# A two-block model kernel: reordering of the first stage (state-space tables, attention heads, modulation weights)

## The reference, cut to what matters

```python
mod = silu(c) @ mod_w[0] + mod_b[0]            # 1024 -> 6*1024
sh1, sc1, g1, sh2, sc2, g2 = split(mod, 6)
h = rms_norm(x, norm_g[0, 0]) * (1 + sc1) + sh1
proj = h @ ab_w_in[0]                          # u (512) and q, k, v (8 heads of 64)
# S5, 2048 complex states: A = exp(dt * a)
#   state[t] = A * state[t-1] + B u[t];  y = Re(C state) + d*u;  y = gelu(y) * sigmoid(...)
# attention: softmax(q k^T / 8 + bias) v, causal, one block of 256
x = x + g1 * (concat(y_ssm, y_att) @ ab_w_out[0])
```

## Time and profile before

| | us |
|---|---|
| median of 3 runs | 1697.28 (1697.18 to 1698.23) |
| the profiled execution, its own time | 1699.96 |
| its span on the core | 1698.2 |
| mean granted TensorE clock | 0.941 |
| front, up to the first product of ab_in | 0 to 51 |
| ab_in loop | 51 to 139 |
| head loop | 139 to 202 |
| glu chunk begins in earnest | 208.86 |

### The profile page before, as it was taken

How to read it: one execution, slowest core, us unless ns; L and a number is a source line. 1 busy time by engine, 2 the same in 40 slices (tenths; PEclk the granted TensorE clock), 3 DMA queues, 4 the chain that set the end, 5 groups by cost and what they waited for, 6 DMA issues and landing times.

```text
span 1698.2 us, 29024 instructions
## 1 busy us (share of the span) xinstructions
PE 1546.5 (91%) x11142; PEld 1395.4 (82%) x11142; DVE 1259.4 (74%) x2002; ACT 746.4 (44%) x987; POOL 52.1 (3%) x38
## 2 busy tenths in 40 slices
PE   4598889999889899999968899889999899889998
PEld 1584479999889799999968565689999778889997
DVE  7998658888989847888964488567666678576665
ACT  2223445444453225444444656454545533254543
POOL 2401100000000000000000000000000000000000
PEclk8698999999999789999979979999999999999999
DMA  8325719878623318777524366435555332235551
GB/s 339 130 94 203 293 50 365 303 289 316 250 88 122 124 50 323 302 303 297 184 108 144 104 213 229 167 115 183 179 191 210 137 124 100 84 123 190 175 195 49
DMA packets 54036, 316.23 MB, mean 186 GB/s; under 512 B 6503, under 2 KB 7560, under 8 KB 28808
## 3 DMA queue, kind: packets, MB, share of 16 engines
q1 hardware_dynamic: 52120, 310.79, 50.2%
q10 hardware_dynamic: 1840, 4.41, 0.9%
HBM read 312.56 MB, written 1.05 MB: 185 GB/s over the span
## 4 chain that ended last, share of the span: by engine, by line
PE 73%; DVE 14%; DMA 4%; issue 4%; ACT 4%; DVEq 1%; POOL 0%; ACTq 0%
PE bank L1841 62%; DMA arena<-in_mod_stream 3%; DVE arena L1143 3%; PE bank L1781 2%; DVE hf L1583 2%; PE bank L2038 2%; DVE rstd L1258 1%; DVE hf L1276 1%; PE bank L2062 1%; PE bank L1795 1%; DVE h_lo L1286 1%; DVE w_lo L1109 1%; ACT w_hi L667 1%; PE bank L1892 1%; PE bank L1807 1%
## 5 line engine op out<-in xcount | busy, mean ns | idle before, releaser
L1841 PE MATMUL bank<-h_hi,w_hi 128*128 128x256 f32 x2184 | 640.6, 293 | 62.1 <-DVE h_lo L1286 55.3
L1841 PE MATMUL bank<-h_lo,w_hi 128*128 128x256 f32 x2184 | 629.2, 288 | 0.0
L1841 PE MATMUL bank<-h_hi,w_lo 128*128 128x256 f32 x2184 | 628.6, 288 | 0.0
L1109 DVE TENSOR_TENSOR w_lo<-raw,w_hi 128x2048 fp32r<-128x2048 f32 x186 | 426.5, 2294 | 135.7 <-ACT w_hi L667 134.9
L1841 PEld LDWEIGHTS bank<-h_hi,w_hi 128*128 128x128 f32 x2184 | 430.3, 197 | 76.1 <-issue 60.3
L1841 PEld LDWEIGHTS bank<-h_lo,w_hi 128*128 128x128 f32 x2184 | 431.1, 197 | 1.1 <-issue 0.7
L1841 PEld LDWEIGHTS bank<-h_hi,w_lo 128*128 128x128 f32 x2184 | 430.6, 197 | 0.0
L667 ACT ACTIVATE w_hi<-raw 128x2048 fp32r<-128x2048 f32 x186 | 355.3, 1911 | 161.9 <-PE bank L1841 152.4
L1841 PE MATMUL bank<-a_hi,w_hi 128*128 128x256 f32 (+1 forms) x760 | 221.6, 292 | 9.9 <-DVE a_lo L1286 3.7
L1841 PE MATMUL bank<-a_lo,w_hi 128*128 128x256 f32 (+1 forms) x760 | 219.3, 289 | 0.0
L1841 PE MATMUL bank<-a_hi,w_lo 128*128 128x256 f32 (+1 forms) x760 | 219.1, 288 | 0.0
(11 more groups left out here) (257 smaller groups left out, 1575.6 us busy)
## 6 DMA issues: line engine op xcount, KB each, us to landing
raw<-in_stream SPq DMA_DIRECT2D x186, 1024.0 KB, 4.9
arena<-in_mod_stream SPq DMA_DIRECT2D x96, 768.0 KB, 6.1
raw<-in_mod_pe SPq DMA_DIRECT2D x36, 512.0 KB, 6.7
arena<-in_ctx_mod SPq DMA_DIRECT2D x8, 1024.0 KB, 5.9
arena<-in_mod_pe SPq DMA_DIRECT2D x12, 512.0 KB, 12.6
sq<-in_bias SPq DMA_DIRECT2D x8, 256.0 KB, 7.2
x<-in_x_t ACTq DMA_DIRECT2D x1, 1024.0 KB, 9.2
arena<-in_ctx_t SPq DMA_DIRECT2D x1, 1024.0 KB, 4.7
```

The lines of the kernel that those rows point to most:

```text
L1109: nc.vector.tensor_tensor(w_lo[s][:], raw[s][:], w_hi[s][:].bitcast(F32), ALU.subtract).then_inc(lo_done, 1)
L1841: ins = nc.tensor.matmul(out_, l, r, start=first and n == 0, stop=last and n == 2, **kw)
```

## The change

1. **Table by recurrence, and on VectorE alone.** `e_pair` now builds only steps 0 to 127 by six instructions over 256 elements. Steps 128 to 255 come from E[t] = 2 cos(64 * angle) * E[t-64] - E[t-128], in four instructions over 128 elements each. The powers shrink with it (six squarings instead of seven, `e1` to 8 entries). All eight pairs are VectorE's: 0 and 1 ahead of the ab_in loop, 2, 3 and 4 at c = 2, 4, 6, and 5, 6 and 7 at h = 1, 3, 5.
2. **All 16 sine products on GpSimd.** `ssm_tile` of tiles 0 to 7 loses L1326; `turned_back(c-1)` comes ahead of `ssm_tile(c)`, and `y_of` has two products for every tile.
3. **Modulation in thirds.** Pieces 0 to 15 as before; 16 to 31 during the ab_in loop, in `hf` and `sq`, two per chunk (four at c = 7); 32 to 47 in the heads, three per head. The bias tiles share `sq` and so are loaded after piece 31. VectorE reads vectors 2 and 3 (`first_mod_out(2, 4)`) between the loops, and `scores(0)` waits for that, since they lie in its bank.
4. **Head step.** VectorE: `head(h)` first, then `ssm_tile(8+h)`, a pair, `recip(h)`, `turned_back(8+h)`. TensorE: `scores(h+1)` first. ScalarE: `probs(h)` at the end of step h.

```diff
         def e_pair(v, link, g):
...
-            v.tensor_tensor(er, a[0], b[0], ALU.mult)
-            link(v.tensor_tensor(part, a[1], b[1], ALU.mult))
-            link(v.tensor_tensor(er, er, part, ALU.subtract))
...
+            er, ei = (t[:, j, 0:T // 2].rearrange("p j (a b) -> p j a b", b=16) for t in (e_re, e_im))
...
+            for q in (2, 3):
+                for k in range(2 * g, 2 * g + 2):
+                    e = [e_all[:, :, k, 64 * (q - i):64 * (q - i) + 64] for i in range(3)]
+                    ins = v.scalar_tensor_tensor(e[0], e[1], cols_[:, 12, k:k + 1], e[2], ALU.mult, ALU.subtract)
+                link(ins)
...
         def _(pool):
-            for g in range(E_POOL, ST // 2):
-                e_pair(nc.gpsimd, link, g).then_inc(sem("e_ready"), 1)
-                pool.wait_ge(sem("e_ready"), g - E_POOL + 1)
-            for j in range(8, ST):
-                pool.wait_ge(sem("scan_done"), j - 7)
+            for j in range(ST):
+                pool.wait_ge(sem("scan_done"), j + 1)
+                if j >= 2:
+                    pool.wait_ge(sem("state_ready"), j - 1)
                 nc.gpsimd.tensor_tensor(by_sin[j % 2], rot_b, e_im[:, j, :].unsqueeze(1).broadcast_to([P, 2, T]), ALU.mult)\
...
             for c in range(8):
                 lo_upto(Q["ab_in"] + c + 3)
+                if c:
+                    turned_back(c - 1)
                 ssm_tile(c)
-                if c in (2, 4):
-                    link(e_pair(nc.vector, link, 1 + c // 2))
-                if c == 6:
-                    y_out(0)
+                if c in (2, 4, 6):
+                    e_pair(nc.vector, link, 1 + c // 2)
+            y_out(0)
+            turned_back(7)
+            first_mod_out(2, 4)
             for h in range(HEADS):
-                if h % 2 == 0:
-                    dve.wait_ge(sem("e_ready"), h // 2 + 1)
+                head(h)
+                if h == 1:
+                    y_out(1)
                 ssm_tile(8 + h)
-                if h == 0:
-                    y_out(1)
+                if h in (1, 3, 5):
+                    e_pair(nc.vector, link, 5 + h // 2)
                 if h == 5:
                     y_out(2)
-                if h == HEADS - 1:
-                    turned_back(8 + h)
-                if h:
-                    recip(h - 1)
-                head(h)
-                if h < HEADS - 1:
-                    turned_back(8 + h)
-            recip(HEADS - 1)
+                recip(h)
+                turned_back(8 + h)
             y_out(3)
-            first_mod_out(2, 6)
+            first_mod_out(4, 6)
...
                 if c >= 2:
                     y_of(c - 2)
+                for m in beside_pieces(c):
+                    pm_piece(m)
+            pm_turn(3)
...
             pe.wait_ge(bank_free, FILL["ab_in"] + 8)
+            pe.wait_ge(sem("mod_read"), 2)
             scores(0)
             for h in range(HEADS):
+                if h + 1 < HEADS:
+                    scores(h + 1)
                 if h + 9 < ST:
                     bu(9 + h)
...
                 if h:
                     head_out(h - 1)
-                if h + 1 < HEADS:
-                    scores(h + 1)
```

More of the change, by code:

```diff
@@ L400, in build @@
             MOD_HALF.append((buf[j % n], landed[j % n], _n_[key], n))
-        pm_landed = [sem(f"pm_landed{i}") for i in range(PM_SLOTS)]
-        PM_PIECE, _n_ = [], [0] * PM_SLOTS
-        for m in range(PM_PIECES):
-            k = m % PM_SLOTS if m < PM_FIRST else (m - PM_FIRST) % PM_LATE
-            _n_[k] += 16
-            PM_PIECE.append(((pm_w if m < PM_FIRST else pm_late)[k], pm_landed[k], _n_[k]))
+        PM_PIECE, _n_ = [], {}
+        for first, last, ring in ((0, PM_FIRST, pm_w), (PM_FIRST, PM_BESIDE, pm_beside), (PM_BESIDE, PM_PIECES, pm_late)):
+            for m in range(first, last):
+                k = (m - first) % len(ring)
+                _n_[k] = _n_.get(k, 0) + 16
+                PM_PIECE.append((ring[k], sem(f"pm_landed{k}"), _n_[k], m - len(ring) + 1 if m >= first + len(ring) else None))
@@ L567, in _ @@
             sp.wait_ge(sem("h_ready"), H[1])
+            for m in range(PM_FIRST, PM_FIRST + 4):
+                load_pm(m)
+            for c, q in enumerate(range(Q["ab_in"] + 6, Q["ab_out"] + 2)):
+                load(q)
+                for m in (2 * c, 2 * c + 1):
+                    load_pm(PM_FIRST + 4 + m)
+            for m in range(PM_FIRST + 14, PM_BESIDE):
+                load_pm(m)
+            sp.wait_ge(sem("pm_used"), PM_BESIDE)
             for h in range(4):
                 load_bias(h)
-            load_plain("ab_in", 6)
-            load_plain("glu")
-            load_plain("ab_out", 0, 2)
             sp.wait_ge(hi_done, Q["ab_out"] + 2)
@@ L782, in _ @@
             for h in range(HEADS):
-                if h:
-                    probs(h - 1)
                 act.wait_ge(sem("peak_ready"), h + 1)
@@ L792, in _ @@
                     probs_copy(h - 1)
-                for g in range(2, 6):
+                for g in (4, 5):
                     if 8 * g + 7 in late_pieces(h):
@@ L797, in _ @@
                     head_copy(h - 1)
+                probs(h)
             for n in range(UT):
@@ L1215, in _ @@
             link(nc.vector.tensor_copy(pows[0][:, 1, :], sn))
-            for k in range(7):
+            for k in range(6):
                 p, p2 = pows[k], pows[k + 1]
@@ L1252, in first_mod_out @@
                 bias = par[:, COL["mod_b"] + c0:COL["mod_b"] + c1]
-                src = half(6, 0) if g0 == 0 else half(4, 1)
-                link(nc.vector.tensor_tensor(mod[:, 0, c0:c1], src[:, c0:c1], bias, ALU.add))
+                src = half(6, 0) if g0 == 0 else half(PM_SUM[g0], 1)
+                nc.vector.tensor_tensor(mod[:, 0, c0:c1], src[:, c0:c1], bias, ALU.add).then_inc(sem("mod_read"), 1)
+                dve.wait_ge(sem("mod_read"), g1 // 2)
             def norm_rstd(n):
@@ L1886, in y_of @@
                     pe.wait_ge(sem("y_ready"), n - 1)
-                c_, s_ = by_cos[j % 2], by_sin[j % 2]
-                terms = [(0, c_[:, 0, :]), (1, c_[:, 1, :])]
-                if j < 8:
-                    terms += [(2, s_[:, 1, :]), (1, s_[:, 0, :])]
-                for i, (e, v) in enumerate(terms):
-                    ins = nc.tensor.matmul(half(Y_BANK[n], 0)[r:r + 32, :], c_turned[:, e, n, r:r + 32], v, start=(i == 0), stop=(i == len(terms) - 1))
+                for e in range(2):
+                    ins = nc.tensor.matmul(half(Y_BANK[n], 0)[r:r + 32, :], c_turned[:, e, n, r:r + 32], by_cos[j % 2][:, e, :],
+                                           start=(e == 0), stop=(e == 1))
                 ins.then_inc(sem("ssm_y_done"), 1)
```

86 lines of the change are left out of this document (37 added, 49 removed).

## The result

The changed kernel took 1707.68 us (median of 13 runs, 1703.06 to 1711.39). The kernel before took 1698.23 us on the same chip (median of 13, 1689.49 to 1704.46). The ratio is 1.0053, with a 95% interval of 1.0036 to 1.007: slower by about 9 us, where 1698.1 with a range of 1691 to 1706 was predicted. The profiled execution took 1708.16 us with a span of 1706.3, so its numbers are set against the 1699.96 and 1698.2 of before.

The account below looks back on a forecast made before the run. VectorE was taken to bound both loops; 16.6 us gained in front were given back as four more pairs (15.2), stalls (9.5) and combining, less savings. Glu comes 0.7 us later, 209.6 against 208.86; total 1698.1 us, range 1691 to 1706.

Parts of the forecast that it names:

- the front: Before the ab_in loop: without GpSimd's table work, w_lo of chunk 1 starts at 47.3 instead of 63.9, 16.6 us gained.
- the stall: Behind by_cos: GpSimd's sine product holds up the following w_lo or pair by 0.95 us, ten times, 9.5 us in all.
- Rival C: ab_in loop and heads: the sine product does not hold up w_lo and pairs, ten stalls go; 1689.5 us, chance 0.11.
- the loops: ab_in and heads: VectorE sets the pace; ab_in steps 7.96 or 11.76 us with a pair, head steps 7.32 or 10.97.
- My sign that it must have no idle time: Both loops: every term counts VectorE as full, so idle time in either would make the prediction wrong as a whole.
- Rival B: Heads: TensorE's clock falls in gaps ahead of heads 2, 4 and 6, so TensorE bounds them; 1703 us, chance 0.20.
- Behind it nothing is edited: Behind the glu chunk's start: no code is changed, so the only question is when that product starts afterwards.
- About 0.2% can be told: Whole kernel: a measurement can tell about 0.2%, 3.4 us.

Follow-up runs that it names:

- a_sin8: The changed kernel with GpSimd's sine product over 8 columns in place of 256 for tiles 2 to 15; 1695.39 us, 0.9967 of before.
- a_no2: The changed kernel with sine products of tiles 0 to 7 on VectorE again and four products per y_of; 1702.04 us, 1.0014 of before.
- a_cm2: The changed kernel with two idle VectorE products (0.9 us) ahead of the w_lo in the conformer's last step; 1702.18 us, 1.0007 of before.
- b_cm5: The kernel before with five idle VectorE products (2.2 us) ahead of the w_lo in the conformer's last step; 1705.63 us, 1.0033 of before.

## Why the prediction was wrong

**Right: the front.** The reciprocal at 37.6 was measured at 37.50, w_lo of chunk 1 at 47.3 at 47.18, the pair of 3.8 at 3.80. The 16.6 us came in full.

**Right: the stall.** 3.26 - 2.29 = 0.97 us for a w_lo and 1.39 - 0.42 = 0.97 for a pair, against 0.95, and a_sin8 shows its cause. On this the rule of the Trainium skill ("SBUF — State Buffer", "SBUF: two separate sides") and the trace agree. Rival C is out.

**Right: the loops, within 1.1 us a row.** Predicted starts of the ab_in steps 62.8, 70.8, 82.5, 90.5, 102.2, 110.2, 122.0; the w_lo stand at 61.74, 70.00, 82.48, 89.50, 102.25, 110.83, 122.61. Scores took 2.04 behind 9.73 us of rest (2.1 predicted). Head 0 came at 133.88 for 133.3, head 7 at 198.09 for 197.9, glu at 210.10 for 209.6. VectorE was the bound, as summed. My sign that it must have no idle time was not met to the letter: in the ab_in loop it waited 1.9 us for `w_hi`, in the heads 2.06 us for `y_of(6)` (1.0 in the sum) and 0.44 us ahead of head 5. What I did not see is that TensorE was just behind: undoing part 2 alone leaves a loop that part 3 holds up equally (a_no2).

**Rival B, in part.** The clock in the heads fell to 0.79, and TensorE worked at 1.2 GHz in several of them. But it held VectorE up by only 2.5 us (2.06 in step 0, 0.44 ahead of head 5), and the head loop took 64.2 us for the 64.6 summed. The trace agrees with what the Trainium skill says in "TensorE: Matmul & The Clock Gate", "HAM oscillation — how this bites in real kernels": work that follows a rest starts at the lower clock (the first scores took 2.04 us behind 9.73 us of rest, others 1.13 at the full clock). What this case adds is the price: 2.5 us in the heads, where VectorE sets the pace, and in the conformer 6.6 us between an early and a late return of the clock.

**Wrong: one sentence.** "Behind it nothing is edited" was taken to mean that everything behind the glu chunk keeps its length. That term was put at 0 and was 6.9 us in the profile. The same instructions took 6.6 us longer in the conformer stage, because the clock came back 15 us instead of 4 us after a rest, and a_cm2 and b_cm5 show that the position of the work decides this, and not what the front leaves behind. The rest of the 6.9 is a sum of smaller moves of both signs (+1.4 up to the feed-forward layer, +1.3 in cm_in, -2.4 in all behind cm_out's second w_lo); most of their places have low clock too, but no run tests them. Of the 9.6 us between 1698.1 and 1707.68 the rest is small: 0.5 at the glu chunk, 1.0 because the median of before moved from 1697.28 (3 runs) to 1698.23 (13 runs), and about 1 between the profiled executions and the medians. The prediction should have carried these moves in its range: the conformer stage of before had a clock of 0.79 with stretches at 0.50, and the kernel before itself spreads from 1689.49 to 1704.46. The range missed by 1.7 us. "About 0.2% can be told" was too hopeful for the same reason: an interval of ten runs is 0.4% wide here.

**What stays open.** Why the new front comes to the conformer stage on the bad side each time, though the clock first falls at another point in each execution (31.5 to 37.5 us). Stages that wait for a rise of the clock may bring the executions back together; this is a guess that no run tests. The stage's length is known from one traced execution of each kernel, and only the medians speak for the others.

## What to carry to other kernels

A sum over the edited stretch can be right to half a microsecond at its end and the total still wrong by nine: wherever TensorE rests and its clock falls, shifting the same code by a microsecond can cost or save six. Look up such stages behind the edit and put their two lengths into the range. Judge an edit by a row at its end (here the first w_lo of ab_out, which itself scatters by up to 2.0 us) and by the median of many runs, and keep the two apart. And when two engines of a loop are both over 90% busy, work moved to either makes the loop longer (8.93 us a step to 9.65 or 10.05): only the part that took work off the shared path (GpSimd's table work out of VectorE's way) was a gain, and it was worth more alone than with the three parts around it.
